# Moving the loads of 48 modulation tiles from SyncE's queue to ScalarE's

## What is computed

```
def first_block(x, ...):
    x = x + (mixers(rms_norm(x)) through branch_a, branch_b) @ w_out      # stage w_out
    h = rms_norm(x, g_ffn)
    x = x + (silu(h @ w1) * (h @ w3)) @ w2                                # stages ffn_up, ffn_down
    x = x + sigmoid(rms_norm(x, g_ple) @ w_ple_gate) * (p @ w_ple)        # stages ple, ple_gate
    return rms_norm(x, g_final)

def second_block(x, c, ...):                # two layers, each a mixer and a PEER feed-forward
    shift, scale, gate = silu(c) @ mod_w + mod_b      # four times; it does not depend on x
    h = rms_norm(x, g) * (1 + scale) + shift
    x = x + gate * mixer(h)
    ...
```

## Time and profile before

| | us |
|---|---|
| runs of the kernel before | 2553.27, 2554.57, 2545.8 |
| median | 2553.27 |
| span of the profiled execution, first to last instruction | 2556.0 |
| PE busy in the span | 2467.2 (97%) |
| stage w_out to the end of ple_gate in that span | about 252 to 545 |

### The profile page before, as it was taken

The page is one execution under the profiler, slowest core; times in us unless marked ns, Lnnn a source line. Parts: engine busy times, 40 slices in busy tenths (PEclk is TensorE's granted clock), DMA queues, the critical chain, the costliest instruction groups (busy, mean ns, idle before and its releaser), DMA issues.

```text
span 2556.0 us, 47107 instructions
## 1 busy us (share of the span) xinstructions
PE 2467.2 (97%) x18074; PEld 2285.6 (89%) x18074; DVE 1823.4 (71%) x3372; ACT 1242.9 (49%) x2142; POOL 1230.2 (48%) x525
## 2 busy tenths in 40 slices
PE   7999899989899999999999999999999999999999
PEld 7998899879799999998888888889999999888887
DVE  6757674467739899996766765662996999655555
ACT  6344443455554544444444455555554444444544
POOL 5547587655569977670000004445997677100000
PEclk8999899999899999999999998999999999999999
DMA  5334586743356655447778763334665555566664
GB/s 170 134 91 157 215 311 230 275 138 107 111 158 200 194 167 156 154 155 247 256 256 262 251 210 100 100 107 148 192 185 174 155 156 157 176 193 191 190 193 145
DMA packets 126062, 457.93 MB, mean 179 GB/s; under 512 B 13984, under 2 KB 15392, under 8 KB 125600
## 3 DMA queue, kind: packets, MB, share of 16 engines
q1 hardware_dynamic: 125424, 450.73, 55.7%
q10 hardware_dynamic: 432, 4.33, 0.4%
HBM read 453.95 MB, written 1.05 MB: 178 GB/s over the span
## 4 chain that ended last, share of the span: by engine, by line
PE 84%; DVE 9%; ACT 2%; issue 2%; DMA 2%; POOL 1%; SPq 0%; DVEq 0%; POOLq 0%; ACTq 0%
PE mm L1311 28%; PE ms L1351 27%; PE mm L829 17%; PE ms L1332 3%; DVE hs L1986 1%; DVE work L1986 1%; PE ms L836 1%; POOL low L1929 1%; DVE scratch L1986 1%; PE ms L844 1%; DVE mm L1980 1%; PE mm L997 1%; DMA ring<-w_ffn_down 1%; PE mm L836 1%; ACT high L1549 0%
## 5 line engine op out<-in xcount | busy, mean ns | idle before, releaser
L1929 POOL TENSOR_TENSOR low<-ring,high 128x1024 fp32r<-128x1024 f32 (+2 forms) x502 | 1216.4, 2435 | 947.0 <-ACT high L1549 783.4
L1794 ACT ACTIVATE high<-ring 128x1024 fp32r<-128x1024 f32 x506 | 535.8, 1059 | 355.4 <-PE ms L1351 317.2
L1311 PE MATMUL mm<-hs,high 128*128 128x256 f32 x4096 | 524.2, 281 | 3.4 <-ACT high L1549 3.4
L1351 PE MATMUL ms<-high,wts 128*128 128x512 f32 x2048 | 510.7, 392 | 0.0
L1311 PEld LDWEIGHTS mm<-hs,high 128*128 128x128 f32 x4096 | 490.3, 188 | 3.8 <-issue 3.8
L2560 DVE TENSOR_TENSOR low<-ring,high 128x1024 fp32r<-128x1024 f32 x256 | 313.4, 1225 | 248.2 <-ACT high L1794 248.1
L1351 PEld LDWEIGHTS ms<-high,wts 128*128 128x128 f32 x2048 | 384.2, 188 | 83.1
L1549 ACT ACTIVATE high<-ring 128x1024 fp32r<-128x1024 f32 (+2 forms) x252 | 258.1, 1030 | 168.1 <-PE mm L829 76.3
L829 PE MATMUL mm<-hs,high 128*128 128x256 f32 x2224 | 293.3, 286 | 8.1 <-ACT high L1549 7.2
L829 PEld LDWEIGHTS mm<-hs,high 128*128 128x128 f32 x2224 | 274.8, 193 | 13.1 <-ACT high L1549 9.2
L1351 PE MATMUL ms<-low,wts 128*128 128x512 f32 x1024 | 276.3, 392 | 3.0 <-DVE low L2560 3.0
(11 more groups left out here) (341 smaller groups left out, 3045.3 us busy)
## 6 DMA issues: line engine op xcount, KB each, us to landing
ring<-w_peer_experts SPq DMA_DIRECT2D x512, 512.0 KB, 3.7
work<-w_mod SPq DMA_DIRECT2D x48, 512.0 KB, 5.3
ring<-w_late_mods SPq DMA_DIRECT2D x48, 512.0 KB, 4.5
ring<-w_ffn_up SPq DMA_DIRECT2D x44, 512.0 KB, 5.5
ring<-w_peer_q SPq DMA_DIRECT2D x32, 512.0 KB, 3.8
ring<-w_fox_in SPq DMA_DIRECT2D x32, 512.0 KB, 3.6
ring<-w_lru_in SPq DMA_DIRECT2D x22, 512.0 KB, 3.5
ring<-w_gates SPq DMA_DIRECT2D x16, 512.0 KB, 3.5
```

The lines of the kernel that those rows point to most:

```text
L1311: ins_ = pe.matmul(mm[:, s_ % BANKS, 0:T], w_[:, k * P:(k + 1) * P], hs[:, b_, k, :], start=pass_ == 0 and k == 0, stop=pass_ == 2 and k = ...
L1351: ins_ = pe.matmul(ms[:, 2 * c + half, :], wts[:, s_ % 3, b_, c * P:(c + 1) * P], v_[:, half * 512:(half + 1) * 512], start=s_ == 0 and pa ...
L1794: act.activation(high[:, (q0 + i) % CUT, :], ring[:, n_ % RAW, :], ACT.Copy) \
L1929: pool.tensor_tensor(low[0:rows, cut_slot, 0:width], ring[0:rows, raw_slot, 0:width], high[0:rows, cut_slot, 0:width].bitcast(F32), ALU.su ...
```

## The change

The 48 loads leave SP's list and are issued by ACT. ACT issues them in `load_mods`, at places of its program where it has just waited for a product to be taken out by DVE; the wait for the slot to be free is still in front of each. The 26 mods that DVE adds in `ffn_up` are spread over places 3 to 21 where they were spread over 0 to 21, and DVE's special case for the first two places goes.

```
+UP_MODS_FROM = 3
...
+for _name, _count, _first, _places, _all in (("w_out", 6, 0, 6, KD), ("ffn_up", 26, UP_MODS_FROM, FFG - UP_MODS_FROM, FFG),
+                                             ("ffn_down", 16, 0, KD, KD)):
+    for _p, _ks in enumerate([[]] * _first + spread(_count, _places) + [[]] * (_all - _first - _places)):
         MODS_BEHIND[_name, _p] = EARLY_MODS[_n:_n + len(_ks)]
         _n += len(_ks)
+        MODS_UP_TO[_name, _p] = _n
...
-    if name in ("w_out", "ffn_up", "ffn_down"):
-        tiles = {"w_out": 1, "ffn_up": 2, "ffn_down": 3}[name]
-        return [tile for p in range(count // tiles) for tile in own[tiles * p:tiles * (p + 1)] + MODS_BEHIND[name, p]]
...
-                for m in MODS_IN_FRONT.get(n, ()):
-                    load_mod(m)
...
+            def load_mods(added):
+
+                while mods_begun[0] < min(added + MOD_RAW, len(EARLY_MODS)):
+                    m = mods_begun[0]
+                    if m >= MOD_RAW:
+                        act.wait_ge(sem("mod_tiles_added"), m - MOD_RAW + 1)
+                    name, i = EARLY_MODS[m]
+                    act.dma_start(mod_ring[:, m % MOD_RAW, :], streams[name][i]) \
+                        .then_inc(sem(f"mod_slot{m % MOD_RAW}_loaded"), 16)
+                    mods_begun[0] += 1
...
             S.did(act.activation(scratch[:, 0:1024], halves, ACT.Square), "head_squares")
+            load_mods(0)
             gates_out(11, 14)
...
                 square(1, k, "w_out")
+                if k:
+                    load_mods(MODS_UP_TO["w_out", k - 1])
                 raw_high(1, k)
...
                     out_taken(act, OUT0["ffn_up"] + 2 * (j - 2) + 1)
+                    load_mods(MODS_UP_TO["ffn_up", j - 2])
...
                 square(2, k, "ffn_down")
+                load_mods(MODS_UP_TO["ffn_down", k - 1] if k else MODS_UP_TO["ffn_up", FFG - 1])
                 raw_high(2, k)
...
             for j in range(FFG):
-                if j > 1:
-                    add_mods("ffn_up", j)
+                add_mods("ffn_up", j)
...
-                if j == 1:
-                    add_mods("ffn_up", 0)
-                    add_mods("ffn_up", 1)
```

More of the change, by code:

```diff
@@ L388 @@
 MODS_BEHIND, _n = {}, 0
-for _name, _count, _places, _all in (("w_out", 6, 6, KD), ("ffn_up", 26, FFG, FFG), ("ffn_down", 16, KD, KD)):
-    for _p, _ks in enumerate(spread(_count, _places) + [[]] * (_all - _places)):
+MODS_UP_TO = {}
+for _name, _count, _first, _places, _all in (("w_out", 6, 0, 6, KD), ("ffn_up", 26, UP_MODS_FROM, FFG - UP_MODS_FROM, FFG),
+                                             ("ffn_down", 16, 0, KD, KD)):
+    for _p, _ks in enumerate([[]] * _first + spread(_count, _places) + [[]] * (_all - _first - _places)):
         MODS_BEHIND[_name, _p] = EARLY_MODS[_n:_n + len(_ks)]
         _n += len(_ks)
+        MODS_UP_TO[_name, _p] = _n
 assert _n == len(EARLY_MODS)
@@ L416, in stage_tiles @@
     return own
[L419 to L425, removed]
+TILES = [_tile for _name, _count, _, _, _ in STREAM for _tile in stage_tiles(_name, _count)]
 TILE_AT = {tile: n for n, tile in enumerate(TILES)}
@@ L1532, in high_parts @@
                     S.did(ins, "h_high")
+            mods_begun = [0]
+            def load_mods(added):
[7 more added lines that the diff above has]
+                    mods_begun[0] += 1
             cuts_made = [0]
```

## The result

The changed kernel takes 2528.78 us (median of 2528.18, 2528.41, 2529.16 and 2530.84); the kernel before, with one more run beside it, 2552.15 us. The ratio is 0.9912, 95% interval 0.9899 to 0.9925: 23 us faster. Measured once more beside other kernels (run e8) it was 0.9922, 0.9907 to 0.9938: 2530.5 against 2551.88 us (medians), 21 us faster. One of the seven executions of e8, the profiled one, took 4058.44 us at a granted clock of 0.56, and it is left out of the ratio and of the median. The profiled execution of the changed kernel is the one of 2528.41 us, with a span of 2526.6.

What follows compares the result with a forecast made beforehand. PE bounds it, idling where weight tiles queue on SP behind mods waiting for DVE. 4.6 + 4.2 + 8.7 - 0.5 = 17.0 us off span 2556.0: 2539.0, median 2536 us; range 2532 to 2545, widest 2527 to 2550.

Steps and rivals of the forecast that it cites:

- w_out, 4.6 us: In w_out, PE's 3.15 us idle time and 1.41 us of slow clock after it go: 4.6 us won, at least 3.2.
- Start of ffn_up, 6.8 - 2.6 = 4.2: Up tile 7 starts 6.8 us earlier, less 2.6 for POOL's third low slowing DVE: 4.2 us won, bounds 1.6 and 6.8.
- ffn_down, 9.4 - 0.7 = 8.7: Six ffn_down groups without waits win 9.4 us, less 0.7 for POOL falling behind: 8.7 us, bounds 6.0 and 10.1.
- Late last mod, 0.5: At the end of ffn_down the last mod delays the last raw part of x: 0.5 us lost, 3 at worst.
- ACT's 48 issues, nothing: 48 mod loads on ACT's queue, 0.33 us each, cost nothing; without cover 16 us.
- Mods from place 3, nothing: In ffn_up, DVE having four adds fewer before up tile 7 is taken out wins nothing by itself.
- Wrong: Signs against the forecast, among them DVE waiting over 2 us for ffn_down mods, or mods landing after 6 us or more.
- slower rival: The loop of mod, DVE and ACT bounds ffn_down, 15 us lost there, 2564 us in all; chance 0.09.
- No change: The order of the queues doesn't matter, asking earlier only lengthens landings: 2553 us, at least 2541; chance 0.13.
- Half given back by DVE and POOL: With weight tiles always there, POOL works without pauses and slows DVE: only 7.8 us won, 2545 us; chance 0.16.

Runs made afterwards that it cites:

- e8: The changed kernel, unchanged, measured again beside other kernels on one chip: 0.9922 of the kernel before, 2530.5 us.
- e3: Kernel before, all mods still on SP, up products' mods from the fourth place, each mod four weight tiles later in SP's list: 0.9922, 2528.92 us.
- e5: Changed kernel, but ACT loads only the last 16 mods (ffn_down), SP the first 32, up products' from the fourth place: 0.995 of the kernel before.
- e10: Changed kernel, with POOL waiting before up tile 5's low part until DVE has made all eight low parts of the normed x: 0.9892, 2524.24 us.
- e1: Kernel before, SP still loading the mods, but those of the up products begin at their fourth place: 0.9988, 2545.06 us.
- e2: Changed kernel, ACT loading the mods, but those of the up products begin at the first place, in the old DVE order: 0.9935 of the kernel before.
- e9: Changed kernel with each mod in two 256 KB half loads, run again beside the changed kernel on one chip: 0.9921, 2531.1 us.
- e6: Changed kernel with each mod in two 256 KB half loads, 96 issues on ACT, on another chip: 0.9939 of the kernel before.
- e7: Changed kernel with two slots for mods in place of three: 1.0018 of the kernel before, 2563.95 us.
- e0: The kernel before, unchanged, profiled once more: span 2549.4 us.
- e11: All mods on SP's queue, four weight tiles later in its list, plus POOL's wait before up tile 5: 0.9899 of the kernel before, 2526.59 us.

## Why the prediction was right

The time, 2528.78 us, lies in the widest range, 2527 to 2550, which was made wider for the spread of the runs of before; it is 7 us below the forecast and 3 us below the forecast's own range, 2532 to 2545. The mechanism was the one named: e3 to e5 show it. By its steps (measured against the two executions of before):

- *w_out, 4.6 us:* 5.6 and 4.0; 0.9 of the 5.6 are the slower clock of the first nine matmuls before. No idle time is left between w_out tile 1 and up tile 4.
- *Start of ffn_up, 6.8 - 2.6 = 4.2:* 5.2 and 5.3. Up tile 5 to 7 went from 315.96 - 302.21 = 13.75 to 304.27 - 297.85 = 6.42 us, 7.3 won; DVE's eight steps went from 6.51 to 8.65, 2.1 lost. Both halves were seen rightly; e10 shows that the lost one is POOL's third `low`, and that it needn't be lost.
- *ffn_down, 9.4 - 0.7 = 8.7:* 10.0 and 10.1, the upper bound; 9.9 of the 10.0 lie in the six groups of the sum. The 0.7 us for a POOL that falls behind wasn't there: PE has no wait in the whole stage.
- *Late last mod, 0.5:* no wait of PE in the changed kernel. Its `ple to lru` is 1.7 us longer, but that of e1 (41.4) is 1.4 longer, where ACT loads nothing, and that of e2 (40.0) isn't: not the change. The margin of the last raw part is 1.6 us.
- *ACT's 48 issues, nothing:* right by the median of e9, which has 96; e6 alone can't tell.
- *Mods from place 3, nothing:* mis-sized as a part. Alone it shortens the start of `ffn_up` by 5.2 us (e1), which the sum counted wholly under ACT's queue; the sum is the same, the shares aren't.

Where the 1.7 us of `ple to lru` lie shows behind a wait of PE in `ple_gate` that the kernels before and after have alike, 2.16 and 2.14 us. In the 6.5 us after it the granted clock was 1.00 before; in the changed kernel it was 0.69 for 5.5 us. The first tile there, before and after:

```profile
523.34 2.18 PE L829 MATMUL mm<-hs,high 128*128 128x256 f32 x16
```

```profile
502.00 3.46 PE L812 MATMUL mm<-hs,high 128*128 128x256 f32 x16
```

The three stages gave 20.8 and 19.4 us, where 17.5 was predicted, inside the bounds; the medians differ by 23 and 21. What is beyond the stages can't be told from the spread of the kernel before, whose median went from 2547.8 to 2552.2 between sets of runs, and to 2558.0 on the other chip; so it counts as luck and not as a success of the sum. `ple` began at 477.6 us, not at 481.8.

One sign was named wrongly. "Wrong" was to be DVE waiting over 2 us for mods in `ffn_down`: it waited up to 4.9 us, the median landing there was 5.8 us, the very border of the slower rival, with single landings of up to 8.0, and nothing was lost: ACT had no wait for DVE at a mod load, and where DVE's wait was longest, DVE took the product 1.0 us after PE had ended it, and PE went on all the same. A wait of an engine with slack is no sign; the sign is PE's row.

*No change* failed: asked for earlier, tiles landed little later or not at all (medians: `w_ffn_up` 4.7 us in place of 5.5, the 512 KB tiles of `w_ffn_down` 4.9 both times, the 384 KB ones 6.0 in place of 5.0), and being asked for earlier outweighed that. The Trainium skill's rule that loads started from several engines share the same 16 DMA engines (DMA: Bandwidth & Descriptors, section "Issuing engines are not separate DMA queues") agrees with e3, where all loads stay on SP and the gain is the same, 0.9922. The forecast of no change that was drawn from it was wrong because what the queue cost was not the starting of loads but the waits in it. *Half given back by DVE and POOL* stayed at 2.1 us. *Slower* did not come, but e7 shows that its loop is real: with one slot less the gain was gone, most of it in the middle of `ffn_up` and not in `ffn_down`.

## What to carry to other kernels

Look at what a queue waits for, not only at what it loads: a load whose wait isn't met holds back all loads behind it, and here it was enough to move it to where its wait is met, on the same queue or on another. When several consumers feed from such a list, give each as many slots as its loop (issue, landing, use) needs at the rate at which it is used, and test the margin by taking one away. Where two engines slow each other on short work that PE waits for, let the one whose result isn't due yet wait.

## What the runs showed of the hardware

- At a granted clock of 1.00 PE has two paces, 2.72 and 2.83 us for a tile of 24 matmuls of 256 columns. A stage can keep one for 60 us and more: the middle of `ffn_up` took 100.6 or 104.6 us, a peer stage's first half 398.6 or 403.9 to 404.3. Both are seen in executions of the same kernel (before and e0, e6 and e9). The pace can also change within a stage: in e10 it did behind a wait of PE of 0.63 us, and in e7 behind waits of 0.5 to 0.7 us. What decides was not found.
- One load costs ACT's queue 0.33 us (median of the 48; the longest entry 0.68), and it runs beside ACT's own work: at 477.36 the square of `x` and the last load begin together. The two half loads of e9's last mod take 0.82 us together.
- DVE's eight subtractions of 128x256 took 8.65 us beside three `low` parts of POOL, 6.51 beside two and 4.35 beside one: each `low` part adds some 2.1 us to them. It repeats: 8.66 to 8.67 us in e1, e2 and e3, 6.51 in e0 and 4.35 in e11. No run shows them beside none.
